# Two-layer encoder trunk: the experts in an order found on chip, 64-slot passes for the three least loaded, and a weight ring of nine slots

## The reference, cut to what matters

```python
def moe_swiglu(h, router, w13, w2):
    t = h.reshape(B * S, D)                       # 256 x 1024
    logits = (t @ router).astype(jnp.float32)     # 256 x 8
    top_val, top_idx = lax.top_k(logits, TOP_K)   # two experts per token
    gate = jax.nn.softmax(top_val, axis=-1)
    combine = jnp.einsum('tk,tke->te', gate, jax.nn.one_hot(top_idx, N_EXPERTS))
    for e in range(N_EXPERTS):                    # w13: 1024 x 7168, w2: 3584 x 1024
        out = out + combine[:, e:e + 1] * swiglu(t, w13[e], w2[e])
```

## Time and profile before

| | |
|---|---|
| median of 3 runs | 1832.61 us (1832.45 to 1833.87) |
| span of the profiled execution | 1837.4 us |
| PE busy | 1787.1 us (97%) |
| DVE busy | 948.7 us (52%) |
| ACT / POOL busy | 349.1 us (19%) / 235.8 us (13%) |
| DMA | 473.62 MB, mean 258 GB/s |
| mixture of experts, first to last expert matmul | about 937 to 1825 us |

### The profile page before, as it was taken

The page is one execution under the profiler, slowest core; times in us unless marked ns, Lnnn a source line. Parts: engine busy times, 40 slices in busy tenths (PEclk is TensorE's granted clock), DMA queues, the critical chain, the costliest instruction groups (busy, mean ns, idle before and its releaser), DMA issues.

```text
span 1837.4 us, 36427 instructions
## 1 busy us (share of the span) xinstructions
PE 1787.1 (97%) x15674; PEld 1173.0 (64%) x15674; DVE 948.7 (52%) x2350; ACT 349.1 (19%) x747; POOL 235.8 (13%) x319
## 2 busy tenths in 40 slices
PE   8999999999999998898999999999999999999998
PEld 5888885788445587887665555555555555555554
DVE  6667653655574567754364345354444544435442
ACT  3234332122012253352110000000000000000001
POOL 2432320100011434433000000000000000000000
PEclk9999999999999999999989999999999999999999
DMA  8552436744631011012479999999999999999994
GB/s 310 184 183 90 140 120 205 247 155 167 200 137 41 6 25 33 11 19 99 172 284 406 396 401 418 401 399 409 409 410 389 417 409 393 418 400 416 403 421 168
DMA packets 137958, 473.62 MB, mean 258 GB/s; under 512 B 30168, under 2 KB 59120, under 8 KB 94784
## 3 DMA queue, kind: packets, MB, share of 16 engines
q1 hardware_dynamic: 133904, 459.82, 64.9%
q0 software_dynamic: 2080, 7.37, 1.2%
q10 hardware_dynamic: 1808, 4.03, 0.6%
HBM read 461.09 MB, written 10.10 MB: 256 GB/s over the span
## 4 chain that ended last, share of the span: by engine, by line
PE 91%; DVE 5%; ACT 2%; DMA 1%; issue 1%; SPq 0%; POOL 0%; DVEq 0%
PE ps L1589 21%; PE ps L812 12%; PE ps L994 11%; PE ps L1597 11%; PE ps L1564 11%; PE ps L866 10%; PE ps L1571 5%; PE ps L1162 2%; PE ps L858 1%; PE ps L1008 1%; PE ps L1523 1%; PE ps L1509 1%; PE ps L886 1%; PE ps L820 1%; DVE arena L2530 1%
## 5 line engine op out<-in xcount | busy, mean ns | idle before, releaser
L1589 PE MATMUL ps<-arena 128*64 128x256 f32 x3584 | 397.1, 380 | 0.0
L1589 PEld LDWEIGHTS ps<-arena 128*64 128x64 f32 x3584 | 256.0, 137 | 150.3 <-issue 29.0
L812 PE MATMUL ps<-arena 128*128 128x128 f32 (+9 forms) x1946 | 279.5, 320 | 20.6 <-DVE arena L2518 9.1
L2824 DVE TENSOR_TENSOR arena<-arena,ps 64x256 f32<-64x256 f32 x168 | 71.3, 425 | 403.7 <-ACT arena L2033 403.6
L812 PEld LDWEIGHTS ps<-arena 128*128 128x128 f32 (+3 forms) x1946 | 222.2, 187 | 73.6 <-issue 39.3
L994 PE MATMUL ps<-arena 128*128 128x256 f32 x952 | 210.7, 379 | 0.1
L1597 PE MATMUL ps<-arena 128*32 128x256 f32 x3584 | 205.0, 381 | 0.0
L2033 ACT ACTIVATE arena<-ps 64x256 f32<-64x256 f32 x168 | 63.2, 376 | 738.9 <-PE ps L1589 554.3
L1564 PE MATMUL ps<-arena 128*64 128x512 f32 x896 | 203.1, 598 | 0.0
L994 PEld LDWEIGHTS ps<-arena 128*128 128x128 f32 x952 | 178.6, 190 | 23.8 <-issue 0.5
L866 PE MATMUL ps<-arena 128*128 128x256 f32 (+1 forms) x714 | 189.1, 425 | 0.0
(11 more groups left out here) (304 smaller groups left out, 1440.0 us busy)
## 6 DMA issues: line engine op xcount, KB each, us to landing
arena<-mw SPq DMA_DIRECT2D x336, 1024.0 KB, 12.0
arena<-wqkv SPq DMA_DIRECT2D x35, 1024.0 KB, 7.3
arena<-fw SPq DMA_DIRECT2D x32, 1024.0 KB, 7.5
arena<-wrkv SPq DMA_DIRECT2D x12, 1024.0 KB, 7.3
arena<-awo SPq DMA_DIRECT2D x4, 1024.0 KB, 6.4
arena<-bwo SPq DMA_DIRECT2D x4, 1024.0 KB, 8.6
xg<-arena POOLq DMA_DIRECT2D x8, 384.0 KB, 9.0
arena<-xg SPq DMA_DIRECT2D x7, 384.0 KB, 17.1
```

The lines of the kernel that those rows point to most:

```text
L812: last = mm(o, a, b, start=(n == 0), stop=(n == len(pairs) - 1))
L1589: last = mm(ps[r, g % 4, 0:256], picked[:, b, k, 0:64], w[:, k, a * 256:(a + 1) * 256], start=(k == 0), stop=(k == KB - 1))
L2824: dve.tensor_tensor(hid_e[RH:P, p % 2, j % 3, :], sg_e[RH:P, j % 2, :], ps[RH:P, bank, 0:256], ALU.mult).then_inc(hide_sb, 1)
```

## The change

1. `turns()`, on DVE after the routing: counts the tokens of each expert, ranks the experts by count (expert 0 is forced to rank 0, since its weights are loaded before the counts are known) and gives each turn an expert by rank: turn 0 to 7 take ranks 0, 5, 1, 2, 6, 3, 4, 7. The places and gates are reordered by turn. SP reads the expert's number for each turn from SBUF and loads from a register address.
2. The turns of rank 5, 6 and 7 (turns 1, 4 and 7) are "light": room for 64 tokens, the pass for slots 64 to 95 is left out on every engine, and each of their up units comes free by itself. A light expert with more than 64 tokens would get a further pass at the end.
3. The ring has nine slots for the experts. Slot 6 lies where the recurrence's loaded parameters were, slot 7 at the transposed input, slot 8 at the space of the final gather (and isn't used by the last expert). Buffers of the recurrence are regrouped so that slots come free one after another, and SP starts each first filling at its own event rather than all at `head_done`.
4. `overflow_list` moves from before expert 0 into turn 1; four semaphores are merged; the recurrence's `gate_params(0)` and `(1)` are issued later (after `rkv_ps` reaches 8), as their buffers moved.

```diff
-RING_SHIFT = tuple(len(range(r, U_QKV, RQ_SLOTS)) - U_QKV // R if r < RQ_SLOTS else -(U_QKV // R) for r in range(R))
+LIGHT = 64
+RANK_AT = (0, 5, 1, 2, 6, 3, 4, 7)
+IS_LIGHT = tuple(r >= 5 for r in RANK_AT)
+ROOM = tuple(LIGHT if a else CAP for a in IS_LIGHT)
...
+        rows_slot, late_slot = m.take(SLOT), m.take(SLOT)
+        ya = rows_slot.rearrange("p (k t d) -> p k t d", k=2, t=T)
+        m = Region(union, 53200)
+        ring += [late_slot, m.take(SLOT), rows_slot]
...
+        in_line = collections.deque((3, 4, 5, 0, 6, 8, 1, 2, 7))
+        for u in range(MOE0, MOE_END):
+            if u == MOE_END - U_EXPERT:
+                in_line.remove(8)
+            slot_in_turn.append(in_line[0])
+            in_line.rotate(-1)
...
+                elif IS_LIGHT[n]:
+                    free[u] = (up_ps, RUNS0[n] + g + 1)
+                else:
+                    free[u] = (up_ps, RUNS0[n] + 3 * (g // 2) + 3)
...
             key_rows(1)
+            sp.wait_ge(za.ps, 2)
+            lora_params(1)
+            sp.wait_ge(rkv_ps, 8)
             gate_params(0)
             gate_params(1)
-            sp.wait_ge(za.ps, 2)
-            lora_params(1)
...
+            def first_free(u):
+                slot = slot_of(u)
+                if slot == 4:
+                    sp.wait_ge(E.ps, chain(NQ - 1, 1, 1))
+                elif slot in (5, 0, 6):
+                    sp.wait_ge(Y.ps, NQ)
+                elif slot == 8:
+                    sp.wait_ge(head_done, NQ + 1)
+                elif slot in (1, 2):
+                    sp.wait_ge(*free[before_it[u]])
+                elif slot == 7:
+                    sp.wait_ge(lg_ps, T)
+            e = 0
+            for u in range(MOE0, MOE_END):
+                n, at = (u - MOE0) // U_EXPERT, (u - MOE0) % U_EXPERT
+                if n and at == 0:
+                    sp.wait_ge(order_ok, 1)
+                    e = sp.value_load(expert_no[0:1, n:n + 1], min_val=0, max_val=EXPERTS - 1)
+                if u < MOE0 + R + 3:
+                    first_free(u)
+                else:
+                    sp.wait_ge(*free[before_it[u]])
+                expert_unit(u, e)
+                if at == 10 and n + 1 < EXPERTS:
                     sp.wait_ge(xg_in, 64)
+                    sp.wait_ge(picked_sb, (n + 1) * 2)
+                    sp.dma_start(xe[0:ROOM[n + 1]], xg[ROWS0[n + 1]:ROWS0[n + 2], :]).then_inc(xe_in, 16)
...
-                        if g % 2:
+                        if g % 2 and not light:
...
+                        if light:
+                            down_halves(g, w, first, end).then_inc(down_ps, 1)
+                        elif end:
...
-            for h in range(2):
-                link(dve.tensor_tensor(comb[:, :, h * EXPERTS + 1:(h + 1) * EXPERTS + 1], logits, top.unsqueeze(2).broadcast_to([P, T, EXPERTS]), ALU.mult))
+            link(dve.tensor_tensor(logits, logits, top.unsqueeze(2).broadcast_to([P, T, EXPERTS]), ALU.mult))
+            def turns():
+                dve.wait_ge(place_ps, 2)
+                link(dve.tensor_copy(counts, ps[:, 6, 0:E]))
+                link(dve.tensor_tensor(keyed, counts, const[:, C_FORCE:C_FORCE + E], ALU.max))
...
+                in_turn(expert_at[:, 0:1], const[:, C_ROW:C_ROW + E].unsqueeze(1))
+                dve.tensor_copy(expert_no, expert_at[:, 0]).then_inc(order_ok, 1)
+                in_turn(place2[:, :, 0:E], p8)
+                link(dve.tensor_copy(p8, place2[:, :, 0:E]))
+                in_turn(comb[:, :, 1:E + 1], logits)
+                link(dve.tensor_copy(comb[:, :, E + 1:2 * E + 1], comb[:, :, 1:E + 1]))
...
             picked_out(1, 0, CAP)
+            turns()
             addresses()
...
-            overflow_list()
+            for n in range(EXPERTS - 1):
+                expert(n, RUNS0[n], IS_LIGHT[n], n * 16 + 16, None, (n + 1) % 2, overflow_list if n == 1 else None)
```

More of the change, by code:

```diff
@@ L8 @@
+import collections
 import math
@@ L72 @@
 OVER = 5
+LIGHT = 64
+RANK_AT = (0, 5, 1, 2, 6, 3, 4, 7)
+IS_LIGHT = tuple(r >= 5 for r in RANK_AT)
+ROOM = tuple(LIGHT if a else CAP for a in IS_LIGHT)
+RUNS_AT = tuple((2 if a else 3) * (GE // 2) for a in IS_LIGHT)
+RUNS0 = tuple(sum(RUNS_AT[:n]) for n in range(EXPERTS + 1))
+RESULTS0 = tuple(2 + sum(1 if a else 2 for a in IS_LIGHT[:n]) for n in range(EXPERTS + 1))
+ROWS0 = tuple(sum(ROOM[:n]) for n in range(EXPERTS + 1))
+FULL = EXPERTS
 C_ID = 0
@@ L231, in build @@
         ones = m.take(P)
+        counts = m.take(EXPERTS)
+        keyed = m.take(EXPERTS)
+        rank = m.take(EXPERTS)
+        turn_of = m.take(EXPERTS, EXPERTS)
+        expert_at = m.take(2, EXPERTS)
+        expert_no = m.take(EXPERTS).bitcast(I32)
         full_e = m.take(4, 2 * EXPERTS)
@@ L328, in build @@
             rowsB.append(m.take(2, RQ))
+        m = Region(after_pads + 6 * KB * S, after_pads + 6 * KB * S + 5 * KB * LORA + KB * LORA)
+        assert m.at <= LATE_AT
+        E2Tm = [m.take(4, P) for _ in range(2)]
+        Rp = [m.take(2, P) for _ in range(2)]
         z0e = [m.take(4, RH) for _ in range(2)]
@@ L377, in mo_of @@
             return mo_late[q % 2][i // 2] if i % 2 else mo_early[i // 2]
-        slot_full = [sem(f"slot_full{i}") for i in range(R)]
+        slot_full = [sem(f"slot_full{i}") for i in range(R + 3)]
         in_x = [sem("in_x0"), sem("in_x1")]
@@ L548, in down_quarter @@
             return unit(DN0 + j)[:, 0:2 * h * D].rearrange("p (k n) -> p k n", n=D)[:, h * i:h * i + h, 512 * n:512 * n + 512]
[L552 to L576, removed]
+        for n, plan in enumerate(plans):
+            for kind, g, u in plan:
+                if kind == "down":
+                    free[u] = (down_ps, n * (GE // 2) + g + 1)
+                elif IS_LIGHT[n]:
+                    free[u] = (up_ps, RUNS0[n] + g + 1)
+                else:
+                    free[u] = (up_ps, RUNS0[n] + 3 * (g // 2) + 3)
+        over_plan = expert_plan(MOE_END)
+        over_uses = [slot_in_turn[MOE_END:].count(r) for r in range(R)]
         def x_scale(t):
@@ L672, in _, with expert_unit @@
                 square(RKV0 + n, wrkv[n // 2, :, (n % 2) * 512:(n % 2 + 1) * 512])
[L674 to L685, removed]
+            def expert_unit(u, e):
+                kind, g, _ = plans[(u - MOE0) // U_EXPERT][(u - MOE0) % U_EXPERT]
+                tiled_unit(u, (mw13 if kind == "up" else mw2)[bass.ds(e, 1), g])
             def tiled_unit(u, w):
@@ L1549, in gather_half, with scatter @@
                 last.then_inc(picked_ps, 1)
-            def scatter(n, b, back, width):
-                pe.wait_ge(y_sb, n * 2 + 4)
+            def scatter(results, b, back, width):
+                pe.wait_ge(y_sb, results)
                 pe.wait_ge(pickT_sb, back)
@@ L1557, in scatter, with expert @@
                     run(ps[:, (4, 7, 0, 1)[k], :], [(pickT[0:width, b, t, :], yb[0:width, h * 512:(h + 1) * 512])]).then_inc(back_ps, 1)
-            def expert(n, c, b, plan, landed, before_last=None):
+            def expert(n, runs, results, light, c, b, plan, landed, before_last=None):
+                per = 2 if light else 3
                 def down_halves(g, w, first, end):
@@ L1643, in landed @@
                     def landed(u):
[L1644 removed]
+                        pe.wait_ge(slot_full[slot_of(u)], j * (32 * over_uses[slot_of(u)]) + 32 * (earlier[u] + 1))
                     n = j + EXPERTS
@@ L1650, in _ @@
                     gather_half(0, 1, CAP, j + 2)
-                    expert(n, n + 1, 0, over_plan, landed)
-                    scatter(n, 0, j + 2, CAP)
+                    expert(n, j * UPS + RUNS0[FULL], j * 2 + RESULTS0[FULL], False, n + 1, 0, over_plan, landed)
+                    scatter(j * 2 + (RESULTS0[FULL] + 2), 0, j + 2, CAP)
         @block.scalar
@@ L2782, in next_picked @@
                 rows = xe[:, 512 * half:512 * half + 512].rearrange("p (k j f) -> p k j f", j=4, f=32)
-                for i in range(CAP // 32):
+                for i in range(room // 32):
                     for j in range(4):
```

270 lines of the change are left out of this document (137 added, 133 removed).

## The result

The changed kernel takes 1808.55 us (median of 4 runs, 1807.33 to 1810.34) against 1832.60, ratio 0.9858, interval [0.984, 0.9876]. A second set of runs, beside runs of the kernel before of its own (1835.36), gave 0.9836 [0.9822, 0.985]. It is 24 to 30 us faster, about half of the 53 us that were forecast, and lies 5.5 us above the range. The direction and the limiter (the supply of weights) were as forecast; the sum for the supply was too small.

What follows compares the result with a forecast made beforehand. DMA's weight supply was to replace TensorE as the bound: 717.3 us from 1047.85 to 1765.2, 0.8 to signal, tail 16.0, clock 2, giving 1784.0, 53.4 below the span before; carried to the median, 1779 us, range 1770 to 1803.

Steps and rivals of the forecast that it cites:

- the sum for the supply: Mixture, from turn 1's start at 1047.85: 693.6 us for 139 units plus token rows, stores and final gather, 717.3 us.
- the 15 us of the three slots: Expert weight ring: three more slots are worth 3 x 4.99 = 15.0 us, only because DMA becomes the bound.
- the harmless edits of the recurrence: Recurrence: gate parameters issued later, after projection 7, have 15 us to spare and cost 0 us.
- the tail: From the last down product's start to the span's end: 17.8 us less the second pass of 1.86, so 16.0 us.
- unit 29 starts its transfer there: Start of turn 1: 21 slots freed plus nine slots, so unit 29 starts and 139 of 168 units are left.
- the scatter done by 954 and the wait covered: Turn 0: rows scattered by about 954; SP's wait has 4 us of cover, otherwise turn 0's full ring hides it.
- Rows at 12.8 + 5.9 + 5.0 = 23.7 us: Supply after turn 1's start: six token-row loads 12.8 us, seven result stores 5.9, final gather 5.0.
- the carrying over: From profiled span to median time: 53.4 us below the span before, taken off the median 1832.6, gives 1779.2.
- supply is slower than I think: Mixture's weight supply: at 407 GB/s 15.4 us more, 1795; up to 1825 if slots aren't refilled in time; 1803 to 1829: 0.09.
- the port's limit: An allowance of 4 us more at the range's fast end; the text given says no more of it.
- The tail at the lower clock: End of the kernel: TensorE's clock may be lower for part of the tail; 2 us in the forecast, 8.7 at the slow end.
- the range's fast end of 1770: Whole kernel: no loss to rows and none to the clock, 710 us and 0 instead of 717.3 and 2.

Runs made afterwards that it cites:

- late_rows: Changed kernel with the load of turn 1's token rows behind the 14th unit of turn 0 instead of the 11th: 1805.44 us, 0.9826 of before.
- rows_cut: Changed kernel with token-row loads for turns 2 to 7 bringing 32 rows instead of 96 or 64 (wrong tokens): 1792.75 us, 0.9759 of before.
- act_heavy: Changed kernel with token-row loads issued by ACT on its own queue and all eight turns heavy: 1836.32 us, 1.0002 of before.
- one_light: Changed kernel with only turn 7 light and the other turns heavy: 1812.51 us, 0.9867 of before.
- six_slots: Changed kernel with a ring of six slots instead of nine, three light turns kept: 1822.73 us, 0.9927 of before.

## Why the prediction was wrong

Right were: the supply is the bound, about 420 GB/s in a backlog (418 from 980 us to the end of turn 0), the 15 us of the three slots, the harmless edits of the recurrence, the clock (0.97 to 0.98 in the light turns), and the tail (15.6 us, against 16.0 and 2 more for the clock). Expert 0 started at 934.4, 2.5 us earlier than the 936.9 that was to hold within 1. The turns: turn 1 took 87.0 us (1045.48 to 1132.48; forecast 73 to 76), turn 4 104.8 (96 to 102), turn 7 105.2 to the end of its last down product, the heavy ones 111 to 115. More than 139 units were still to come at the start of turn 1. The windows over turns 4 and 7 have 410 and 395 GB/s, not 415 to 420.

The step that failed is the supply's sum of 717.3 us from the start of turn 1; the profiled execution needed 744.6 (1045.5 to 1790.1). Its terms, as the prediction put them:

- "Until then 21 slots have come free ... unit 29 starts its transfer there": 26.8 units had landed, so 141.2 were left, not 139: 11 us. The first refills met the scatter of 2 MB and SP's wait for it, and DMA gained back only the 0.27 us a unit by which it is faster than a heavy turn. The prediction had the scatter done by 954 and the wait covered; the rows were ready in time (943.64), but SP's wait lasted until 963.05, and late_rows puts its price at 2 to 6 us. A slot that is free is not a slot that is filled; I had not drawn DMA's line through turn 0.
- A unit of 5.01 instead of 4.99 us: 3 us.
- Rows at 12.8 + 5.9 + 5.0 = 23.7 us: 37.2. The six row loads lost 19.8 us by the packets of the trace, where I had 12.8: 3.1 to 4.2 for 96 rows (I had 2.4) and 2.4 to 2.5 for 64 (1.6). I had priced all by the load in the earlier trace rows, which was one of the two cheapest of its trace (2.4; the seven lost 2.2 to 3.4). Scaling by rows was right, as rows_cut shows; the price that I scaled was too low. Stores, gather and the remaining units were about as put; the last unit came 4.7 us late, a term that I didn't have.

Start and tail gave back 5 us of these. The rest of the miss is the carrying over: the execution of before that was profiled is 4.8 us longer in span than its median run, while those of the changed kernel have spans 1.6 us shorter than their times. So the profile of before showed an execution some 6 us slower than its median run, and I took 4.8 us off for it, which the changed kernel's profile gives no ground for. Together: 11 + 3 + 13.5 - 5 + 6.4, and 0.8 less for the landing that 1790.1 holds already and 1.2 for the median above the profiled run, 29.3 us, which is what was missed.

The rival "supply is slower than I think" is what came true: 1795 at the 407 of a whole expert, and up to 1825 if the slots aren't refilled in time. I gave the stretch from 1803 to 1829 a chance of 0.09 because I took the 407 of the earlier trace rows for TensorE's pace alone. It was that; but supply with dear rows needs 109 to 110 us a turn, as the changed kernel shows, and that is within 1 to 2% of TensorE's 110.7.

Two terms of the range are shown by no run. For the port's limit and its "4 more" there is no figure here: the supply moved 418 to 424 GB/s in its windows without a row load, and 429 in the highest window here, the changed kernel's 955 to 960 us. The tail at the lower clock, with 2 us in the forecast and 8.7 more in the slow end, was my estimate; a clock of 0.50 stands in the earlier trace rows, at 930 to 935 us before expert 0, while the tail of the changed kernel had 1.00 up to 1800 us.

Two small slips bore on nothing: the DMA slices are at nine tenths from the 22nd on, not the 21st, and the range's fast end of 1770 is 1779.2 less 7.3 and 2 alone, without those "4 more".

## What to carry to other kernels

When work goes from one engine and leaves a second limit 1% behind, sum the second line whole, from its first refill, with every small transfer at the price that the weights around it pay. The gain then is the distance between the two lines, not the work left out: 111.7 us went, 24 to 30 came, and one light turn gave nearly as much. And follow the lead through the turns, not only the totals: what the second line could win in a slow stretch it can't keep beyond the slots that there are. Look next for what shortens the new line: here a queue of their own for the small loads, 12 to 16 us for four lines moved.

## What the runs showed of the hardware

The DMA share doesn't tell a supply that sets the pace from one that is held to TensorE's. In act_heavy, where TensorE never waits for weights in this stretch, it is 1.00 at 404 GB/s, in one_light, where it doesn't either, 1.01 at 407, and in the changed kernel, where it does (1.1 us), 1.01 at 407, all three between 1160 and 1270 us:

```profile
1160.00:1270.00 110.00, 110.00 (x1226) 59.70 (x1224) 49.36 (x163) 9.09 (x23) 0.00 (x0) 1.00 1.00 404
```

```profile
1160.00:1270.00 110.00, 110.00 (x1226) 59.69 (x1224) 48.43 (x162) 8.13 (x23) 0.00 (x0) 1.00 1.01 407
```

```profile
1160.00:1270.00 110.00, 108.93 (x1224) 59.29 (x1222) 48.26 (x159) 9.11 (x23) 0.00 (x0) 1.00 1.01 407
```

What tells them apart is TensorE's wait for weights. The issuer's wait for slots doesn't: it is 522 us in six_slots, where TensorE waits 83 us for weights, and 25 us in the changed kernel, where TensorE waits 68.8. The median time to landing of a load of 1 MiB was 11.8 us in act_heavy, 18.3 in six_slots and 26.9 in the changed kernel.

SP's issues took longer as well. The weight loads of 1 MiB take it 1.99 us each in the changed kernel (median) and 0.33 in six_slots. The row loads of the changed kernel, issued by SP (duration in ns, least, median, most), take 2067 where those of before took 450; on ACT's queue they take 349:

```profile
L806 SPq DMA_DIRECT2D arena<-xg x7: 368/2067/3007, 963.0 to 1599.4; - x7
```

```profile
L765 SPq DMA_DIRECT2D arena<-xg x7: 428/450/457, 964.4 to 1630.2; - x7
```

Whether these longer issues cost time no run here separates. From six to nine slots, with three light turns in both, the median time to landing rose from 18.3 to 26.9 us; whether a tenth slot would put more under way wasn't run.
